# Up projections of the four feed-forwards: the weights' high part multiplied by n_high and n_rest in one product of 512 columns

## The reference

```python
def swiglu_2(h, w1, w3, w2):
    return (jax.nn.silu(h @ w1) * (h @ w3)) @ w2

h = h + swiglu(rms_norm(h, ffn_norm_g[i]), w_gate[i], w_up[i], w_down[i])
...
x = x + g_f * swiglu_2(modulate(rms_norm_2(x, norm_ffn[l]), sh_f, sc_f), w_ffn1[l], w_ffn3[l], w_ffn2[l])
```

## Time and profile before

| | us |
|---|---|
| median of 3 runs | 2433.05 |
| lowest and highest | 2419.49, 2437.21 |
| profiled execution, its own time | 2428.65 |
| span of its profile, first to last instruction | 2426.9 |

### The profile page before, as it was taken

The page is one execution under the profiler, slowest core; times in us unless marked ns, Lnnn a source line. Parts: engine busy times, 40 slices in busy tenths (PEclk is TensorE's granted clock), DMA queues, the critical chain, the costliest instruction groups (busy, mean ns, idle before and its releaser), DMA issues.

```text
span 2426.9 us, 42031 instructions
## 1 busy us (share of the span) xinstructions
PE 2214.3 (91%) x17189; PEld 2063.5 (85%) x17189; DVE 1616.7 (67%) x2073; ACT 1006.5 (41%) x1189; POOL 203.1 (8%) x194
## 2 busy tenths in 40 slices
PE   8896998899999888899999779899999977989998
PEld 6674888799999878899999668899999966888998
DVE  8885554565588876655578877565457896856554
ACT  4112445444344454433444355343344435534332
POOL 3761001100000110000000110000000011000000
PEclk9998999999999999999999889999999989999999
DMA  7676664566554433465555223455545432334652
GB/s 241 245 281 247 213 222 156 191 193 205 174 170 157 139 105 122 131 199 190 172 178 162 87 70 105 137 158 189 191 141 176 146 104 70 105 105 140 190 177 84
DMA packets 290144, 392.49 MB, mean 162 GB/s; under 512 B 8311, under 2 KB 256461, under 8 KB 283342
## 3 DMA queue, kind: packets, MB, share of 16 engines
q1 hardware_dynamic: 285620, 383.53, 48.4%
q10 hardware_dynamic: 3546, 5.80, 0.8%
q0 software_dynamic: 832, 1.08, 0.2%
HBM read 387.14 MB, written 3.15 MB: 161 GB/s over the span
## 4 chain that ended last, share of the span: by engine, by line
PE 74%; DVE 15%; ACT 4%; issue 3%; DMA 2%; POOL 1%; DVEq 0%; ACTq 0%; SPq 0%
PE L L848 59%; PE M L848 3%; DVE w_rest L431 3%; PE L L1102 2%; PE L L1088 2%; PE M L985 2%; DVE m L1960 1%; DVE n_rest L1969 1%; ACT w_high L425 1%; DVE work L2482 1%; PE M L1338 1%; DVE work L2459 1%; DVE work L2587 1%; PE L L1115 1%; DVE rstd L1957 1%
## 5 line engine op out<-in xcount | busy, mean ns | idle before, releaser
L848 PE MATMUL L<-n_high,w_high 128*128 128x256 f32 x3424 | 977.7, 286 | 35.4 <-DVE w_rest L431 15.1
L848 PE MATMUL L<-n_rest,w_high 128*128 128x256 f32 x3424 | 961.4, 281 | 0.0
L848 PE MATMUL L<-n_high,w_rest 128*128 128x256 f32 x3424 | 960.9, 281 | 0.0
L431 DVE TENSOR_TENSOR w_rest<-raw,w_high 128x2048 fp32r<-128x2048 f32 x293 | 671.5, 2293 | 252.7 <-PE L L848 245.9
L425 ACT ACTIVATE w_high<-raw 128x2048 fp32r<-128x2048 f32 x293 | 560.9, 1915 | 415.1 <-PE L L848 380.2
L848 PEld LDWEIGHTS L<-n_high,w_high 128*128 128x128 f32 x3424 | 655.6, 191 | 57.5 <-issue 40.0
L848 PEld LDWEIGHTS L<-n_rest,w_high 128*128 128x128 f32 x3424 | 654.9, 191 | 0.6
L848 PEld LDWEIGHTS L<-n_high,w_rest 128*128 128x128 f32 x3424 | 654.3, 191 | 0.0
L848 PE MATMUL L<-hid_high,w_high 128*128 (+1 forms) x704 | 196.5, 279 | 6.1 <-DVE hid_rest L2384 6.1
L848 PE MATMUL L<-hid_rest,w_high 128*128 (+1 forms) x704 | 195.5, 278 | 0.0
L848 PE MATMUL L<-hid_high,w_rest 128*128 (+1 forms) x704 | 195.5, 278 | 0.0
(11 more groups left out here) (395 smaller groups left out, 2784.1 us busy)
## 6 DMA issues: line engine op xcount, KB each, us to landing
raw<-in_w_in SPq DMA_DIRECT2D x116, 1024.0 KB, 5.4
raw<-in_w_ffn SPq DMA_DIRECT2D x99, 1024.0 KB, 5.3
raw<-in_w_ada SPq DMA_DIRECT2D x32, 1024.0 KB, 6.2
raw<-in_w_out SPq DMA_DIRECT2D x16, 1024.0 KB, 4.9
raw<-in_w_gate SPq DMA_DIRECT2D x11, 1024.0 KB, 5.3
raw<-in_w_up SPq DMA_DIRECT2D x11, 1024.0 KB, 5.4
raw<-in_w_down SPq DMA_DIRECT2D x11, 1024.0 KB, 4.9
work<-in_w_ada SPq DMA_DIRECT2D x8, 1024.0 KB, 7.3
```

The source lines that it names most:

```text
L431: nc.vector.tensor_tensor(w_rest[:, u.first % 2, :], raw[:, u.first % 4, :], w_high[:, u.first % 4, :].bitcast(F32), ALU.subtract).then_in ...
L848: ins = mm(dst, a, b, start=first and i == 0, stop=last and i == 2, skip_group_check=skip)
```

## The change

n_high and n_rest become the two halves of one tile, `n_both`. In `ffn_up` each block of weights takes two matmuls instead of three: w_high by both halves side by side, 512 columns into a full PSUM bank (columns 0 to 255 high x high, 256 to 511 high x rest), then w_rest by n_high, added to the first 256 columns of the bank. So the sum over the three parts is no longer complete in PSUM; the two halves of a bank have to be added outside.

- A unit fills two banks instead of one, a pair four. Even pairs go to M, odd pairs to L. TensorE waits at the first unit of pair p (from the third on) for `hid_ready` of pair p - 2.
- ScalarE copies the second halves of a unit's two banks into `gate` (`half_out`, one copy a unit); once VectorE has added the first halves it takes Silu in place, from SBUF (`silu_of`).
- VectorE adds the first halves for the gate unit (`gate_sum`) and for the up unit (`up_pair`), then multiplies, rounds and makes the rest. The work on a pair is spread over the two units behind it, each time behind the split of the next unit's rest.
- The loops of ScalarE and VectorE over `ffn_up` are written out; TensorE writes out the first four and the last two units.
- The last pair (number 10) lies in M, so the down projection begins when the last but one pair is ready; the last one is waited for ahead of unit 9 of 11. The context's transposes move behind its first unit, and VectorE's copies of them behind its second split there.

```diff
-        n_high = sb("n_high", [P, DC, T], F32R)
-        n_rest = sb("n_rest", [P, DC, T], F32R)
+        n_both = sb("n_both", [P, 2, DC, T], F32R)
+        n_high, n_rest = n_both[:, 0, :, :], n_both[:, 1, :, :]
...
+            def up_unit(u, j, chunk=None):
+                pe.wait_ge(rest_ready, u.count(1))
+                wh, wr = parts(u, DC)
+                pair_banks = M if j % 4 < 2 else L
+                for c, o in ([(c, o) for c in range(DC) for o in range(2)] if chunk else [(c, o) for o in range(2) for c in range(DC)]):
+                    if chunk and o == 0:
+                        chunk(c)
+                    bank = pair_banks[:, j % 2 * 2 + o, :]
+                    mm(bank.rearrange("p (s t) -> p s t", s=2), wh[:, c, o * P:(o + 1) * P], n_both[:, :, c, :],
+                       start=c == 0, stop=False, skip_group_check=True)
+                    ins = mm(bank[:, 0:T], wr[:, c, o * P:(o + 1) * P], n_high[:, c, :],
+                             start=False, stop=c == DC - 1, skip_group_check=True)
+                ins.then_inc(unit_done, 1)
...
-                cols_linear(pre + "ffn_up", chunk=normed_chunk(k))
-                if pre == "":
+                up_linear(pre, normed_chunk(k))
+                pairs = FC // 2 * (HID_OF[pre] + 1)
+                def context_turned():
                     pe.wait_ge(ctx_in, 16)
+                    pe.wait_ge(hid_ready, pairs)
                     turn_tokens(rows_m, turned)
-                pe.wait_ge(hid_ready, FC // 2 * (HID_OF[pre] + 1))
...
+                pe.wait_ge(hid_ready, pairs - 1)
+                acc_linear(pre + "ffn_down", hid_high, hid_rest, before={9: last_pair},
+                           behind_first=context_turned if pre == "" else None)
...
+                def half_out(p, x):
+                    act.wait_ge(unit_done, first + 2 * p + x + 1)
+                    if p >= 2 and x == 0:
+                        act.wait_ge(hid_ready, base + p - 1)
+                    half, dst = set_of(p, x)
+                    A(dst, half, ACT.Copy).then_inc(up_half, 1)
+                def silu_of(p):
+                    act.wait_ge(up_sum, base + p + 1)
+                    sg = set_of(p, 0)[1]
+                    A(sg, sg, ACT.Silu).then_inc(up_act, 1)
...
+                def up_pair(p):
+                    dve.wait_ge(up_half, 2 * base + 2 * p + 2)
+                    sg, hh = gates_of(p)
+                    link(V.tensor_tensor(hh, sums_of(p, 1), hh, ALU.add))
+                    dve.wait_ge(up_act, base + p + 1)
+                    link(V.tensor_tensor(hh, sg, hh, ALU.mult))
+                    high = hid_high[:, 2 * p:2 * p + 2, :]
+                    link(V.tensor_copy(high, hh))
+                    V.tensor_tensor(hid_rest[:, 2 * p:2 * p + 2, :], hh, high.bitcast(F32), ALU.subtract).then_inc(hid_ready, 1)
+                for j in range(cnt):
+                    ahead_rest(dve, Unit(first + j), UNITS)
+                    if j % 2:
+                        gate_sum(j // 2)
+                    elif j:
+                        up_pair(j // 2 - 1)
+                up_pair(cnt // 2 - 1)
```

More of the change, by code:

```diff
@@ L114, in _number_units @@
             uses = [x + 1 for x in uses]
+        elif name.endswith("ffn_up"):
+            pass
         elif name == "glu":
@@ L941, in acc_unit, with up_linear, acc_linear @@
                 ins.then_inc(unit_done, 1)
-            def acc_linear(name, xh, xr, before={}):
+            def up_unit(u, j, chunk=None):
[11 more added lines that the diff above has]
+                ins.then_inc(unit_done, 1)
+            def up_linear(pre, chunk):
+                name, base = pre + "ffn_up", FC // 2 * HID_OF[pre]
+                first, n = FIRST[name], COUNT[name]
+                for j in range(4):
+                    if j == 2:
+                        for b in range(4):
+                            pe.wait_ge(bank_free[b], BANK_USES[name][b])
+                    up_unit(Unit(first + j), j, chunk if j == 0 else None)
+                with pe.Fori(0, n // 4 - 1) as i:
+                    for j in range(4):
+                        if j % 2 == 0:
+                            pe.wait_ge(hid_ready, base + 2 * i + j // 2 + 1)
+                        up_unit(Unit(first + 4 + j, i), j)
+                for j in range(n // 4 * 4, n):
+                    if j % 2 == 0:
+                        pe.wait_ge(hid_ready, base + j // 2 - 1)
+                    up_unit(Unit(first + j), j)
+            def acc_linear(name, xh, xr, before={}, behind_first=None):
                 first, n = FIRST[name], COUNT[name]
@@ L1751, in feed_forward @@
                 base = FC // 2 * HID_OF[pre]
[L1753 to L1764, removed]
@@ L1766, in feed_forward @@
-                first, n = FIRST[pre + "ffn_up"], COUNT[pre + "ffn_up"]
[L1768 to L1771, removed]
-                        one(j, k2, u)
-                for j in range(4):
-                    step(Unit(first + j), j, j)
-                with act.Fori(0, n // 4 - 1) as i:
-                    for k2 in range(4):
-                        ahead_high(act, Unit(first + 4 + k2, i), UNITS)
-                        if k2 % 2 == 0:
-                            act.wait_ge(unit_done, Unit(first + 4 + k2, i).count(1))
-                            act.wait_ge(hid_ready, base + 2 * i + 2 + k2 // 2 - 1)
-                            A(gate[:, 2 * k2:2 * k2 + 2, :].rearrange("p a t -> p (a t)"), L[:, k2, :],
-                              ACT.Silu).then_inc(up_act, 1)
@@ L2389, in turn @@
-                def turn(i):
-                    for k2 in range(4):
-                        u = Unit(first + k2, i)
-                        ahead_rest(dve, u, UNITS)
-                        if k2 % 2:
-                            dve.wait_ge(unit_done, u.count(1))
-                            pair(i, k2, base + 2 * i + k2 // 2 + 1, steps + 4 * i + 2 * (k2 // 2))
-                turns = cnt // 4
-                with dve.Fori(0, turns) as i:
-                    turn(i)
-                n[0] += 4 * turns
@@ L2400, in feed_forward, with sums_of, gates_of @@
[L2400 to L2406 removed]
+                def sums_of(p, x):
+                    return (L if p % 2 else M)[:, 2 * x:2 * x + 2, 0:T]
+                def gates_of(p):
+                    return gate[:, p % 2 * 4:p % 2 * 4 + 2, :], gate[:, p % 2 * 4 + 2:p % 2 * 4 + 4, :]
@@ L2419, in feed_forward @@
+                for j in range(COUNT[name]):
+                    ahead_rest(dve, Unit(FIRST[name] + j), UNITS)
+                    if j in beside:
+                        beside[j]()
                 dve.wait_ge(unit_done, FIRST[name] + COUNT[name])
```

61 lines of the change are left out of this document (26 added, 35 removed).

## The result

The changed kernel takes 2437.3 us in the median of 20 runs (2430.1 to 2444.7), the kernel before 2431.4 in 20 runs taken with it. The ratio is 1.0029 with a 95% interval of 1.0017 to 1.0042: 0.3% slower, some 7 us, where I had forecast 14.5 us less. The interval is clear of no change, so the sign of my forecast is wrong. The time lies just inside my range (2403 to 2438), by luck: the upper end of the range was the price of rival B, not of the mechanism I forecast.

What follows compares the result with a forecast made beforehand. The prediction took TensorE's matmuls to bound the kernel; 9.1 us (merging) plus 5.4 (ends) plus 0 (VectorE and ScalarE work) made 14.5 less, from 2433.05 to a median of 2418.5 us, range 2403 to 2438.

Steps and rivals of the forecast that it cites:

- rival B: Up projections: a wide float32r matmul costs 235 ns; 5.3 us slower (2438.4), or 18.5 with upper levels (2451.5); chance 11%.
- Term 1: Merged matmul in 21 of 22 up-projection units: 6.8 ns fixed cost saved in each of 1344 blocks, 9.1 us less.
- rival C: Up projections: cost goes by columns alone, merging wins nothing, only the ends count; 5.4 us less, 2427.7; chance 13%.
- Rival A: Up projections: the weight load bounds narrow matmuls and a wide one hides it; 26 us less, 2407; chance 27%.
- Term 2: End of each up projection: TensorE goes on to the down projection without waiting for the last pair; 5.4 us less together.
- Term 3: Up projections: more work on VectorE and ScalarE per pair, hidden behind TensorE's matmuls; cost 0.
- Rival D: Up projections: VectorE's longer row holds back a split; at 3.6 us more per pair 40 us, 2458; chance 4%.
- three low and one high: Up-projection stages: three at 114.4 us, the last at 118.8, assumed to stay so; each stage at the upper level costs 4.4.

Runs made afterwards that it cites:

- ends_only: The kernel before with only the early start of the down projection, three matmuls of 256 columns kept: 2423.9 us, ratio 0.9970 to the kernel before.
- split_wide: The changed kernel with each matmul of 512 columns made of two of 256, everything else kept: 2421.2 us, ratio 0.9961 to the kernel before.
- ends112: ends_only with n_high and n_rest 112 instead of 48 words behind the weights: 2421.0 us, ratio 0.9958 to the kernel before.

## Why the prediction was wrong

**Term 1 is the step that failed.** I took the 6.8 ns above the columns (6.7 by the starts) for a fixed cost of each matmul, and so 220 ns for the wide one and 333.6 a block. Measured in the kernel: 235 and 353.3. It is not a cost of the matmul: a wide one has twice that extra even in the best case, 226.7 ns, which is two narrow ones at their best. So there was nothing to win from the start; the 9.1 us had no source. That part is rival C, whose 227 ns was the price of the wide one at its best place.

**It is worse than nothing** because of two things in which the merged stream differs from the narrow one, each of them worth 6.7 ns a block here: the wide matmul costs more at the place at which n lies (233 instead of 227 at 48 words), and a change of width with every matmul costs by itself (353 instead of 346.7 when grouped). Together 353.3 against 340.0, 1344 x 13.3 = 17.9 us, less the share of stages that were at the upper level before: with 13 of 16 at the lower one 14.5 us. Less the 7.3 of the early start this makes 7 us slower, which is what was measured. It is rival B, with its price of 235 ns, which the earlier trace rows had shown; B's sum without the levels was 117.1 us a stage, measured are 118.7, since the narrow matmul beside the wide one costs 118 and not 113.5. I had set that row aside because "in those short bursts everything is slower than in a long stream", and took only the difference to the earlier trace rows, 5 to 10 ns in favour of merging. The long streams at 48 words later gave 233 as well. Whether the scores were slower than the up stages through the place of their own operands or for being short, no run shows; their operands lie elsewhere, and a difference between two forms at one place says nothing about another.

**Rival A falls.** It rested on the weight load bounding the narrow matmuls. The streams of 128 and 192 columns put what is likely the load at 112 ns, just under 113.3; but a wide matmul, which leaves twice the time for a load, costs twice as much, so nothing was held back by it. The Trainium skill (TensorE: Matmul & The Clock Gate, Back-to-back issue gap) gives about 216 ns for 512 columns, between single matmuls; the best stream of float32r here has 226.7, so it does not hold for these streams. By the same rule 256 columns take about 109 ns, and a block would go from 327.5 to 325.0: an estimate from that page is thus 2.5 ns a block, and not the 12.0 of this rival, as the prediction has it. Its section LDWEIGHTS (loading the stationary operand) has the columns divided by 1.2, an estimate of 107 ns for 128; the shortest distance in these streams, with a load ahead of each matmul, is 112.

**Term 2 was right.** Forecast 5.4; the hand-overs of the profile give 6.0, and by itself the early start gains 7.3 us (2 to 12 by its interval). What I had not seen is that without a wait the down projection starts at the level of the up projection, which in the changed kernel is always the upper one. It keeps it only for its first unit (0.2 us), because the short wait at the second one draws anew. The first and the second down unit of the second feed-forward in the profile after, 47 distances each, 117.7 and 113.4 ns:

```profile
1153.87:1159.40 5.53, 5.53 (x49) 1.00 0.22 92
1159.90:1165.23 5.33, 5.33 (x48) 1.00 0.85 275
```

In the other three it is 117.8 in both, in the first of them with the transposes in between and no wait.

**Term 3 was right.** VectorE's busy time rose by 61.4 us (1616.7 to 1678.1), 61 by my count; the chain behind the last unit took 1154.07 to 1157.30, 3.23 us against 3.25; no wait inside the stages. The copies cost 0.573, not 0.60. Rival D did not happen.

**The levels.** I had left "three low and one high" and said that no row tells why. In the narrow form they change from execution to execution, in the changed one they don't, so the fair comparison is 340 in most stages against 353 in all. What sets the level, why the place of the operands matters and why turning widths costs, these runs don't show. The most frequent costs are 6.7 ns a block apart (340, 346.7, 353.3, 360), but at other places there are 350, 351 and 356 as well.

**Better than both kernels** are ends_only (0.9970), split_wide (0.9961) and ends112 (0.9958): the part of the change that looked like its by-product, the early start of the down projection, without the merging. Their intervals overlap, so no one of them is the best by these runs.

## What to carry to other kernels

Before merging matmuls to save a cost "per matmul", measure a stream of each width, and the mix that the kernel will have: if two narrow ones cost what a wide one does, there is nothing to save, and the number of instructions is no measure. Measure it with the operands where the kernel has them, since a shift of the moving tile (n, which streams through the weights) by a few words changes the price of the same stream, over all places tried by up to 6%, and the best place differs from form to form. And split a change into its parts on the chip: here one part lost some 16 us and another, meant as an aside, won 7.

## What the runs showed of the hardware

- float32r matmuls of 256 columns cost 113.3 to 120.0 ns (340 to 360 for three), by the distance of the moving tile (0 to 240 words tried). At odd multiples of 16 words they are at 113.3 or 117.8, varying from one stream to the next; in the kernels a level stayed until a wait or other work came between, with one exception.
- 512 columns cost 226.7 ns at 0 words and 233.3 at 48, 384 columns 173.3, 320 columns 147. 128 and 192 columns both cost 112 ns, with a load of 128 x 128 weights ahead of each.
- 512 and 256 columns by turns cost 346.7 to 354 ns in 79 of 80 streams, never the 340 that both widths have alone at their best.
- Behind a wait of 3.33 us ahead of the down projection TensorE's clock was at 1.2 GHz, in four of four, which cost 1.75 us more each; behind the kernel before's wait of 1.97 us it stayed at 2.4 GHz.
